# A decoder layer's expert rows on one core: weighing gathered rows in 32x32 instead of 64x64 squares of the PE array

## What is computed

```
def token_block(args):
    xc, ec, gc = args
    a = jax.nn.gelu(jnp.einsum('cd,ced->ce', xc, u[ec]).astype(jnp.float32), approximate=False)
    return jnp.einsum('ce,ced->cd', gc * a, v[ec].astype(jnp.float32))
```

## Time and profile before

| | us |
|---|---|
| median of 3 runs | 939.04 |
| lowest, highest | 938.22, 941.38 |
| profiled execution, as timed | 938.43 |
| its span in the profile | 936.6 |
| PE busy / DVE / ACT / POOL | 816.7 / 641.4 / 418.1 / 391.8 |
| mean granted clock of TensorE | 0.957 |

### The profile page before, as it was taken

One profiled execution on the slowest core, in us unless ns is written; L12 is line 12 of the kernel. 1 busy time (PEld: TensorE's weight loads), 2 busy tenths in 40 slices (PEclk: granted clock), 3 DMA queues, 4 the chain that ended last, 5 costly groups with the idle time before them and its releaser, 6 DMA issues.

```text
span 936.6 us, 15313 instructions
## 1 busy us (share of the span) xinstructions
PE 816.7 (87%) x5608; PEld 520.3 (56%) x5608; DVE 641.4 (68%) x1450; ACT 418.1 (45%) x1074; POOL 391.8 (42%) x307
## 2 busy tenths in 40 slices
PE   9999999999998877878879998888787879989965
PEld 8999998799976524434336664443333323333311
DVE  5433686465567997879898998778777644444555
ACT  5434565544574664545544454433333322222342
POOL 1000065140004487366455354457558654344560
PEclk9999999999999999899899999979889789999988
DMA  8898533257336999999999999999999999999992
GB/s 303 230 220 209 191 120 136 90 226 260 145 113 233 347 399 415 392 420 415 415 399 385 417 406 389 386 368 395 389 379 397 417 402 417 415 404 409 384 405 103
DMA packets 55026, 303.17 MB, mean 324 GB/s; under 512 B 11515, under 2 KB 14959, under 8 KB 21777
## 3 DMA queue, kind: packets, MB, share of 16 engines
q0 software_dynamic: 37152, 225.29, 60.0%
q1 hardware_dynamic: 14968, 74.03, 21.7%
q10 hardware_dynamic: 2832, 2.88, 2.3%
HBM read 343.80 MB, written 1.54 MB: 369 GB/s over the span
## 4 chain that ended last, share of the span: by engine, by line
PE 46%; DMA 32%; DVE 8%; ACT 6%; issue 5%; POOL 2%; POOLq 0%; SPq 0%; DVEq 0%; ACTq 0%
DMA arena<-in_experts,arena 22%; PE y L1208 11%; DMA late_ring<-in_experts,arena 6%; PE ps L822 6%; PE ps L823 6%; PE ps L824 6%; PE ps L1258 5%; DVE late_ring L2246 3%; DMA rowsT<-in_experts,arena 2%; PE y L1291 2%; DVE w_lo L1813 2%; ACT diag L1619 1%; POOL arena L2454 1%; DMA late_ring<-in_experts,expert 1%; PE ps L865 1%
## 5 line engine op out<-in xcount | busy, mean ns | idle before, releaser
L2246 DVE CUSTOM_DVE_ANT_0 late_ring<-arena 128x1024 f32<-128x1024 f32 x158 | 193.0, 1223 | 105.4 <-DMA arena<-in_experts,arena 102.3
L2454 POOL DMA_INDIRECT arena<-in_experts,arena x148 | 197.0, 1331 | 161.9 <-PE ps L1211 127.3
L1208 PE MATMUL y<-arena,diag 64*64 64x512 f32 x600 | 160.7, 660 | 53.9 <-ACT diag L1619 53.7
L1211 PE MATMUL ps<-arena,diag 64*64 64x512 f32 x616 | 162.9, 652 | 0.0
L1605 ACT ACTIVATE acts<-dots 128x2 f32<-128x2 f32 x125 | 25.4, 203 | 301.0 <-DVE dots L2246 300.6
L1813 DVE TENSOR_TENSOR w_lo<-raw,w_hi 128x2048 fp32r<-128x2048 f32 x36 | 84.9, 2361 | 72.5 <-ACT w_hi L1385 72.5
L2246 DVE CUSTOM_DVE_ANT_0 late_ring<-late_ring,arena 128x1024 f32<-128x1024 f32 x82 | 99.7, 1219 | 39.0 <-DMA late_ring<-in_experts,arena 36.6
L1208 PEld LDWEIGHTS y<-arena,diag 64*64 64x64 f32 x600 | 38.7, 141 | 145.2 <-ACT diag L1619 86.8
L2454 POOL DMA_INDIRECT late_ring<-in_experts,arena x63 | 83.6, 1327 | 79.0 <-PE ps L1211 68.1
L1208 PE MATMUL y<-late_ring,diag 64*64 64x512 f32 x328 | 84.9, 640 | 34.9 <-ACT diag L1619 34.6
L1385 ACT CAST w_hi<-raw 128x2048 fp32r<-128x2048 f32 x37 | 70.5, 1905 | 61.2 <-DMA raw<-in_panels 47.9
(11 more groups left out here) (358 smaller groups left out, 1766.0 us busy)
## 6 DMA issues: line engine op xcount, KB each, us to landing
raw<-in_panels SPq DMA_DIRECT2D x40, 1024.0 KB, 5.1
arena<-in_panels SPq DMA_DIRECT2D x6, 1024.0 KB, 6.8
x<-in_up SPq DMA_DIRECT2D x10, 512.0 KB, 8.0
late_ring<-in_up SPq DMA_DIRECT2D x10, 512.0 KB, 8.0
x<-in_experts SPq DMA_DIRECT2D x10, 512.0 KB, 7.9
late_ring<-in_experts SPq DMA_DIRECT2D x10, 512.0 KB, 7.9
arena<-line_scratch ACTq DMA_DIRECT2D x8, 320.0 KB, 8.1
arena<-in_experts,arena POOLq DMA_INDIRECT x148, 18.6
```

Source lines behind the costliest of these rows:

```text
L1208: straight = pe.matmul(y[rows, t, cols], diag[rows, a % DIAGS, rows], slot(a)[rows, down], start=False, stop=False, skip_group_check=True)
L1211: across = pe.matmul(ps[to, half, :], diag[rows, b % DIAGS, rows], slot(b)[rows, down], start=first, stop=False, skip_group_check=True)
L2246: i = nc.vector.tensor_tensor_reduce(row if n < len(FIRST_BUFFERS) else products[s % GROUP], row, h_rows[:, u // PEER_HEADS, :], 1.0, 0.0, ...
L2454: nc.gpsimd.indirect_dma_start(out=slot(n), out_offset=None, in_=experts, in_offset=bass.IndirectOffsetOnAxis(ap=expert_rows(u)[:, s:s + 1 ...
```

## The change

Squares of 32x32 in place of 64x64. A diagonal matrix has four such squares. Three placements ("band orders") are used: straight (band i into band i), crossed by 2 (band i into band i XOR 2) for the accumulator `ps` half 0, and crossed by 1 (band i into i XOR 1) for `ps` half 1. `y` has two halves as well, and they take the straight placement. Which row and half of a pair goes where depends on whether the group's number is even or odd. `CROSSED_BY` holds the two orders. The semaphore `slot_free` is incremented by the last matmul that reads each row.

```
+BAND = 32
+CROSSED_BY = (2, 1)
...
+            def weigh(into, by, at, row, down, first=False):
+
+                for i in range(P // BAND):
+                    rows, to = band(i), band(i ^ by)
+                    mm = pe.matmul(into[to], at[rows, rows], row[rows, down], start=first, stop=False,
+                                   skip_group_check=True)
+                return mm
+
             def use_pair(t, i, first):

                 pe.wait_ge(diag_ready, i + 1)
                 a, b = i * GROUP, i * GROUP + 1
-                for half in range(2):
-                    cols = slice(half * 512, (half + 1) * 512)
-                    down = slice(D + half * 512, D + (half + 1) * 512)
-                    for rows in (low_half, high_half):
-                        straight = pe.matmul(y[rows, t, cols], diag[rows, a % DIAGS, rows], slot(a)[rows, down],
-                                             start=False, stop=False, skip_group_check=True)
-                    for rows, to in ((low_half, high_half), (high_half, low_half)):
-                        across = pe.matmul(ps[to, half, :], diag[rows, b % DIAGS, rows], slot(b)[rows, down],
-                                           start=first, stop=False, skip_group_check=True)
-                straight.then_inc(slot_free, 1)
-                across.then_inc(slot_free, 1)
+                at_a, at_b = diag[:, a % DIAGS, :], diag[:, b % DIAGS, :]
...
+                if i % 2 == 0:
+                    weigh(y[:, t, halves[0]], 0, at_a, slot(a), downs[0])
+                    weigh(ps[:, 0, :], CROSSED_BY[0], at_b, slot(b), downs[0], first)
+                    last_a = weigh(ps[:, 1, :], CROSSED_BY[1], at_a, slot(a), downs[1], first)
+                    last_b = weigh(ps[:, 1, :], CROSSED_BY[1], at_b, slot(b), downs[1])
+                else:
+                    weigh(y[:, t, halves[1]], 0, at_a, slot(a), downs[1])
+                    last_a = weigh(ps[:, 0, :], CROSSED_BY[0], at_a, slot(a), downs[0], first)
+                    weigh(ps[:, 1, :], CROSSED_BY[1], at_b, slot(b), downs[1], first)
+                    last_b = weigh(ps[:, 0, :], CROSSED_BY[0], at_b, slot(b), downs[0])
+                last_a.then_inc(slot_free, 1)
+                last_b.then_inc(slot_free, 1)
```

More of the change, by code:

```diff
@@ L521, in slot, with band @@
             return at_buffer(buffer_of(n))
-        low_half, high_half = slice(0, P // 2), slice(P // 2, P)
+        def band(i):
+            return slice(i * BAND, (i + 1) * BAND)
         crossed = raw[:, (RAW_LOADED.index("qpeer4") + 1) % RAW_RING, 0:D]
@@ L1203, in use_pair @@
                 a, b = i * GROUP, i * GROUP + 1
-                for half in range(2):
-                    cols = slice(half * 512, (half + 1) * 512)
-                    down = slice(D + half * 512, D + (half + 1) * 512)
-                    for rows in (low_half, high_half):
-                        straight = pe.matmul(y[rows, t, cols], diag[rows, a % DIAGS, rows], slot(a)[rows, down],
-                                             start=False, stop=False, skip_group_check=True)
-                    for rows, to in ((low_half, high_half), (high_half, low_half)):
-                        across = pe.matmul(ps[to, half, :], diag[rows, b % DIAGS, rows], slot(b)[rows, down],
-                                           start=first, stop=False, skip_group_check=True)
-                straight.then_inc(slot_free, 1)
-                across.then_inc(slot_free, 1)
+                at_a, at_b = diag[:, a % DIAGS, :], diag[:, b % DIAGS, :]
+                halves = [slice(half * 512, (half + 1) * 512) for half in range(2)]
+                downs = [slice(D + half * 512, D + (half + 1) * 512) for half in range(2)]
+                if i % 2 == 0:
[10 more added lines that the diff above has]
+                last_b.then_inc(slot_free, 1)
             def sum_crossed(t, halves):
@@ L1220, in sum_crossed @@
                     cols = slice(half * 512, (half + 1) * 512)
-                    for rows, to in ((low_half, high_half), (high_half, low_half)):
+                    for i in range(P // BAND):
+                        rows, to = band(i), band(i ^ CROSSED_BY[half])
                         mm = pe.matmul(y[to, t, cols], ident[rows, rows], crossed[rows, cols],
@@ L1226, in use_alone @@
             def use_alone(t, n, at):
[L1228 to L1233, removed]
+                straight = weigh(y[:, t, 0:512], 0, at, slot(n), slice(D, D + 512))
+                across = weigh(ps[:, 1, :], CROSSED_BY[1], at, slot(n), slice(D + 512, 2 * D))
                 return straight, across
```

## The result

The changed kernel takes 944.1 us (median of 12 runs, 940.51 to 947.08) beside 939.83 us of the kernel before in the same runs: ratio 1.0040, 95% interval 1.0024 to 1.0056. It is 0.4% slower, where 934.8 us was forecast. The profiled execution has a span of 939.1 us (940.93 us as timed), 2.5 us more than before. Measured twice more, on other chips, it came to 1.0037 (1.0017 to 1.0057) and 1.0066 (1.0046 to 1.0086).

The account below looks back on a forecast made before the run. DMA bytes set the floor, with the stage 5% above it because POOL's gathers wait for PE to free buffers. Terms -2.6 - 1.7 + 1.0 - 0.4 + 0.1 (tail) = -3.6 us gave 934.8 us, range 929 to 944.

Parts of the forecast that it names:

- I cost them at nothing.: PE's pairs: weight loads, doubled in number but half as wide, cost nothing, up to another 0.05 us per pair.
- term 2: 480 to 595 us, PE-bound: two double pairs save 1.7 us (0 to 3.4), added starts cost 1.0 us (0 to 2).
- Term 1: 595 to 760 us: rows freed earlier let POOL issue gathers 0.8 us earlier, -2.6 us (0 to -5.3).
- 0.8 us of 25: 595 to 760 us: a buffer comes round every 25 us, so 0.8 us earlier is 3.2%, 5.3 us; half taken.
- bytes decide everywhere: Gather stage: DMA bytes are the bound, so gathers sent earlier only queue longer; about 938.4 us, chance 0.27.
- Term 3: 309 to 480 and 764 to 897 us, PE partly idle and DMA full: -0.4 us (+1 to -3).
- Three streams: PE's pairs: a row band feeds only two squares, so a pair takes three rounds; about 952 us, chance 0.11.
- one bank at a time: PE's pairs: row bands writing the same bank must take turns; about 1,440 us, chance 0.01.
- The clock: 595 to 760 us: PE's clock falls more often, so more pairs run at 1.2 GHz; about 944 us, chance 0.08.
- what I did not see: Whole kernel: the share left for causes not thought of, no size given, chance 0.03.

Follow-up runs that it names:

- n256: The kernel before, 64x64 squares and release kept, each matmul of a pair cut into two of 256 columns: ratio 1.0036.
- early64: The kernel before, 64x64 squares and same number of instructions, but a pair's first row takes the whole first round and is freed earlier: ratio 1.0006.
- the late release: The changed kernel with both rows of a pair freed by the last set, against the kernel before: ratio 1.0074 on one chip, 1.0061 on another.
- after_third: The changed kernel as it is, run again on another chip, against the kernel before: ratio 1.0066.
- half32: The kernel before's 64x64 squares for the first row tile, the changed kernel's 32x32 squares for the second: ratio 1.0021.
- late_third: The changed kernel with both rows of a pair freed by the last set, run beside after_third, against the kernel before: ratio 1.0061.
- n256_first: The kernel before, each matmul of a pair cut into two of 256 columns in the first 20 pairs only: ratio 1.0003.
- n128: The kernel before, each matmul of a pair cut in four of 128 columns, a square's four parts one behind another: ratio 1.193.
- after_again: The changed kernel as it is, run again beside the first experiments on the same chip, against the kernel before: ratio 1.0037.
- n128_turns: The kernel before, each matmul of a pair cut in four of 128 columns, with the squares taking turns: ratio 1.0108.

## Why the prediction was wrong

**The step that failed: "I cost them at nothing."** The added matmuls and loads of weights were priced by their place on PE's array, and there they are indeed almost free (0.02 to 0.03 us a pair, see term 2). That 32 more instructions per pair cost something by their number was in no term. The changed kernel lost 3.5 to 6.2 us in its three measurements; 16 packets at 0.27 us are 4.3. n256 shows that the number alone makes 1.0036, with the squares and the release of before. Whether they cost by being fetched or by being handled stays open, as said above; the row that could have raised the question was on the page of before (44 packets for `q8 instruction`).

**Term 1, the earlier release, -2.6 us (ends 0 and -5.3): worth less than was forecast, and nothing that stands out.** early64 gives +0.6 us (-0.8 to +2.1); against the late release the changed kernel was 3.5 us faster on one chip and 0.5 us slower on another. POOL's waits for PE in 595 to 760 did not get shorter: 48.3 us in all, 49.0 before. The two larger of three rows of after's waits (us in total, times, longest; 33.6 for `arena` is more than in the earlier trace rows, what `late_ring` lost is as much):

```profile
POOL arena L2468 <- PE ps L1209: 33.6, 21, 3.9
...
POOL late_ring L2468 <- PE ps L1209: 8.5, 6, 3.3
```

The mechanism is real: row a is freed 0.79 us ahead of row b, 0.06 us before the change. The step that fails is "0.8 us of 25". The gathers issued in 595 to 760 with the median us to landing: before; after_third and half32, with the early release; late_third, with the late one. The trace of after records too few landings.

```profile
arena<-in_experts,arena POOLq DMA_INDIRECT x52, 15.8
arena<-in_experts,arena POOLq DMA_INDIRECT x53, 16.9
arena<-in_experts,arena POOLq DMA_INDIRECT x54, 17.1
arena<-in_experts,arena POOLq DMA_INDIRECT x53, 15.8
```

With the early release a gather lands 1.1 to 1.3 us later. This fits a gather that, sent earlier, stands longer in a queue that is at 0.99. It is not seen by much: the six other kernels with the late release whose traces have these landings lie between 15.9 and 16.8 us. The prediction had named this sign, a longer landing, for its rival "bytes decide everywhere". The rival had this much right; its 938.4 us are too few because it, too, left the instructions out.

**Term 2, -1.7 for two double pairs and +1.0 for starts: mis-sized.** The double pair at 508.45 saved 0.48 us, not 0.86. A lone pair and the product took 5.53 us before. The chain of after, in order of time (start us, us, what):

```profile
487.35 0.89 PE ps L1209 x16
488.24 3.65 PE ps L1272 x16
492.88 0.91 PE ps L1209 x16
493.79 3.65 PE ps L1272 x16
```

493.79 - 488.24 = 5.55 us: the added starts cost 0.02 us a pair, not 0.05. Both errors are below 2 us together.

**Term 3, the rest, most of it the last stretch, -0.4 (ends +1 and -3): not confirmed.** Rows 192 to 240 took 128.9 us, 126.9 before. But n256_first, which is before's kernel there, took 128.5, so this difference cannot be put down to the edit.

**Rivals.** Three streams, and one bank at a time, fell with the twelve starts within 0.1 us. By the Trainium skill, "TensorEngine Tiling (Array Packing)", Gotcha 1, different row tiles can't write one bank at the same time; the trace disagrees: it has four of them starting on y within 0.03 us (502.90 to 502.93), a lone pair of 1.97 us (1.95 before), and the kernel's time is nowhere near 1,440 us. The clock: 0.89 over 595 to 760 as before, so it did not fall. That its 944 us are the measured time is luck, since its reason did not occur. The range's upper end was set by that rival and lay at the measured median; it had no part for a cost that I had not priced except 3% for what I did not see.

## What to carry to other kernels

When a stage is bound by DMA, count the instructions that an edit adds: here each 254 or so on PE cost some 0.27 us, 1 ns apiece, though the engine ran them in idle squares. Cut work into more instructions only if what that wins is on the path, and test the count alone (the old kernel with its matmuls cut in two) before the new layout. An earlier release won nothing that shows here, where a transfer sent earlier landed later. Don't look for a difference of 2 us of the medians in two traces, which differ by as much at one place by chance. When small matmuls go to several squares, let the squares take turns in the program: with eight matmuls in a row on one square it cost 181 us, with four in a row turns saved nothing.

## What the runs showed that I had not expected

- The price of a packet of PE's instructions, above: some 0.27 us where its bytes are worth 0.04.
- Eight matmuls in a row on one square keep the others waiting: 4.54 us for a pair (n128) against 1.98 us with the same instructions in turns.
- A wait on a semaphore that has long been reached takes time: some 0.08 us for an instruction of two, on PE (5.22 us for 64).
- 12 squares of 32x32 started within 0.1 us, 7 ns from one to the next, four of them on the same bank.
- In some traces PE's records stand ahead of what PE had done. In after_again PE and then ACT read

```profile
336.61 0.44 PE L1148 MATMUL ps<-ident,qpT 128*128 128x128 f32 x2
...
342.14 1.08 PE L1209 MATMUL y<-late_ring,diag 32*32 32x512 f32 x4 [5.10 <-ACT diag L1633]
```
```profile
339.34 0.37 ACT L1646 COPY qpT<-ps 128x256 f32<-128x256 f32 x1 [4.67 <-remote]
```

  ACT waits for nothing but that transpose, which by its record ended at 337.05; the semaphore came at 339.32. There were 30 to 45 such late completions (0.4 to some 2.6 us), by how they are matched, in the trace of after and as many in this one, but 4 in after_third, which is the same kernel, and none in n128_turns, which has more instructions. So they are not what the changed kernel loses by; what they are stays open. They do mean that a single trace can mislead by 2 us at one place, which is how I came to look at the beginning of the stage.
